# Eight modulation blocks multiplied inside the recurrent scan instead of in the readout after it, and the readout's squares on ScalarE

## What is computed

```python
def adaln(cond, w, b):
    return jnp.split(jax.nn.silu(cond) @ w + b, 6, axis=-1)
...
        h_l = modulate(x, sh_a, sc_a)
...
        x = x + gt_a * o_l
        x = x + gt_m * squared_relu_mlp(modulate(x, sh_m, sc_m), mlp_w1[layer], mlp_w2[layer])
```

```python
    def step(s, inp):
        rt, wt, kt, vt, at, bt = inp
        sa = jnp.einsum('bhij,bhj->bhi', s, at)
        s = s * wt[:, :, None, :] + sa[..., None] * bt[:, :, None, :] + vt[..., None] * kt[:, :, None, :]
        y = jnp.einsum('bhij,bhj->bhi', s, rt) if with_out else None
...
        mean = jnp.mean(y, axis=-1, keepdims=True)
        var = jnp.mean(jnp.square(y - mean), axis=-1, keepdims=True)
        y = ((y - mean) * lax.rsqrt(var + RW_GN_EPS)).reshape(r.shape) * lnx_w + lnx_b
        return ((y + bonus) * g).astype(h_l.dtype) @ w_o
```

## Time and profile before

| | us |
|---|---|
| median of 3 executions | 3275.87 (3272.88 to 3277.51) |
| the profiled execution | 3276.72 |
| its span, first to last instruction | 3274.6 |
| scan, first matmul to last result | about 998 to 1527 |
| readout, to the first matmul of the phase after it | 1527 to 1576.4 |

### The profile page before, as it was taken

How to read it: one execution, slowest core, us unless ns; L and a number is a source line. 1 busy time by engine, 2 the same in 40 slices (tenths; PEclk the granted TensorE clock), 3 DMA queues, 4 the chain that set the end, 5 groups by cost and what they waited for, 6 DMA issues and landing times. The chain is left out here.

```text
span 3274.6 us, 79289 instructions
## 1 busy us (share of the span) xinstructions
PE 2935.4 (90%) x35148; PEld 1967.2 (60%) x35148; DVE 1331.3 (41%) x2021; ACT 948.7 (29%) x1646; POOL 314.5 (10%) x253
## 2 busy tenths in 40 slices
PE   7988899999997788787899988798999998998996
PEld 5865577888575666665799877675333333333332
DVE  3355544333763654555455676464110110110112
ACT  3124433222343333432444563432100100100101
POOL 0021200000321122122000002310000000000001
PEclk9999899999998999999899998988999999999997
DMA  7262412222153100003555432088999999999996
GB/s 267 78 243 78 171 52 103 99 82 103 64 195 114 55 23 23 29 29 109 211 180 181 158 129 81 9 293 306 374 421 421 421 422 421 421 422 421 421 422 265
DMA packets 195063, 681.03 MB, mean 208 GB/s; under 512 B 25616, under 2 KB 40464, under 8 KB 145312
## 3 DMA queue, kind: packets, MB, share of 16 engines
q1 hardware_dynamic: 175328, 651.93, 51.2%
q10 hardware_dynamic: 18336, 21.21, 1.8%
q0 software_dynamic: 1152, 4.19, 0.4%
HBM read 651.86 MB, written 25.43 MB: 207 GB/s over the span
## 5 line engine op out<-in xcount | busy, mean ns | idle before, releaser
L4006 PE MATMUL experts_psum_gu<-ring,experts_x 128*32 128x512 f32 x3840 | 431.4, 597 | 34.6 <-DMA ring<-in_w_gu 34.6
L4128 DVE TENSOR_SCALAR experts_gate<-experts_psum_gu 128x768 f32<-128x768 f32 (+1 forms) x32 | 26.4, 824 | 850.2 <-PE experts_psum_gu L4006 850.2
L4006 PEld LDWEIGHTS experts_psum_gu<-ring,experts_x 128*32 128x32 f32 x3840 | 111.9, 110 | 336.2 <-issue 241.5
L4035 PE MATMUL experts_psum_down<-down_weights,experts_hiddenT 128*32 128x256 f32 x4096 | 231.2, 381 | 15.6 <-DMA down_weights<-in_w_down 12.7
L4035 PEld LDWEIGHTS experts_psum_down<-down_weights,experts_hiddenT 128*32 128x32 f32 x4096 | 127.5, 110 | 128.1 <-DMA down_weights<-in_w_down 32.9
L4072 ACT ACTIVATE experts_sigmoid<-experts_gate 128x768 f32<-128x768 f32 (+1 forms) x32 | 23.6, 737 | 584.9 <-DVE experts_gate L4128 584.9
L991 PE MATMUL mlp_psum_bank<-mlp_x_high,mlp_w_high 128*128 128x512 f32 (+1 forms) x512 | 175.5, 343 | 7.1 <-DVE ring_rounded L315 4.5
L315 DVE TENSOR_TENSOR ring_rounded<-ring,mlp_w_high 128x1024 fp32r<-128x1024 f32 x128 | 156.8, 1225 | 44.4 <-ACT mlp_w_high L310 44.4
L991 PE MATMUL mlp_psum_bank<-xT_rounded,mlp_w_high 128*128 128x512 f32 (+1 forms) x512 | 173.5, 339 | 0.0
L1001 PE MATMUL mlp_psum_bank<-mlp_hidden_high,mlp_w_high 128*128 128x512 f32 (+1 forms) x512 | 172.2, 336 | 1.2 <-ACT mlp_relu L937 1.2
L991 PE MATMUL mlp_psum_bank<-mlp_x_high,ring_rounded 128*128 128x512 f32 (+1 forms) x512 | 173.1, 338 | 0.0
(11 more groups left out here) (793 smaller groups left out, 6052.5 us busy)
## 6 DMA issues: line engine op xcount, KB each, us to landing
ring<-in_w_gu SPq DMA_DIRECT2D x192, 1024.0 KB, 25.9
down_weights<-in_w_down SPq DMA_DIRECT2D x96, 1024.0 KB, 27.2
ring<-in_ada_w SPq DMA_DIRECT2D x72, 1024.0 KB, 10.8
ring<-in_mlp_w SPq DMA_DIRECT2D x64, 1024.0 KB, 7.0
xT<-in_w_gu SPq DMA_DIRECT2D x64, 1024.0 KB, 26.0
ring<-in_w_in SPq DMA_DIRECT2D x24, 1024.0 KB, 6.4
spare_unit<-in_w_down SPq DMA_DIRECT2D x16, 1024.0 KB, 27.1
x<-in_w_down SPq DMA_DIRECT2D x16, 1024.0 KB, 27.3
```

What stands on the lines that cost most here:

```text
L4006: mm = nc.tensor.matmul(pg[32 * j:32 * j + 32, gr, :, :], x, strip(w, j), start=False, stop=(u == U - 1))
L4035: mm = nc.tensor.matmul(pd[32 * c:32 * c + 32, gr, :], hidT[:, a, gr, GROUP * v:GROUP * v + GROUP], w[:, a, C * c:C * c + C], start=(v == ...
L4128: v.tensor_scalar(G, pg[:, 0:groups, 0, :], SWI_LIMIT, None, ALU.min).then_inc(s_gt, 1)
```

## The change

The class `ScanModulate` splits a modulation block into products, copy, fold and keep, and the scan calls these at fixed places. Block 0 is multiplied at the start while the first tile is prepared; block i + 1 is multiplied in the `carry` of step i, between L2217 and L2225. ScalarE copies its result behind its copies of W. The fold of block i is issued at the head of the next `totals`, or at k = 2 of the last step, and ScalarE keeps the folded columns at k = 2. TensorE waits for the copied row at the end of `carry`, and for the kept columns before `cumulate`. SyncE issues one ring unit behind the v load of each step from step 1 on, and one more at the end, so that the next phases' first three units (two of w_o, one of the MLP) are also loaded during the scan.

In the readout the eight blocks go. `ModulateBias` loads the bias behind the other loads and adds it between the reciprocal and the token work. The two squares move from VectorE to ScalarE. The `keep_busy` matmuls go to a bank of their own, six at the start and eight between the two turned tiles.

Apart from that, `keep_busy` is taken out of `gemm_feat` (5 matmuls; it runs as "about" and "rwout"), `mlp` (2 + 4; it runs twice), `ab_merge` (4) and `gemm_rows` (5; "mixout").

```diff
@@ -628,7 +628,6 @@
                     if kt == KT - 1:
                         ring.mark(mm)
 
-                keep_busy(g, banks[:, 0, 0:256], 5)
                 for c in range(CHUNKS):
                     ring.take(pe)
                     for kt in range(KT - 2):
...
                                            ALU.add).then_inc(self.s_end, 1)
+        dve.wait_ge(self.s_end, len(self.parts))
+
+
+class ScanModulate:
+
+
+    def __init__(self, g, ph, parts, each):
+        self.g, self.ring, self.each = g, g.ring, each
+        self.dst = [(g.mods[layer % 2], 4 * f, layer) for layer, first, n, _ in parts for f in range(first, first + n)]
+        self.row = ph.sb("mod_row", [P, each, 512])
+        self.s_row, self.s_fold, self.s_kept = ph.sem("mod_row"), ph.sem("mod_folded"), ph.sem("mod_kept")
+        self.done0 = self.ring.done
+
+    def products(self, pe, n, dst):
+        wv = self.ring.take(pe)
+        for kt in range(KT):
+            j = 32 * (kt % 4)
+            if kt == KT // 2:
+                self.ring.wait(pe, self.ring.used - 1, 1)
+            mm = self.g.nc.tensor.matmul(dst[j:j + 2, :], self.g.silu[:, self.dst[n][2] // 2, kt, :], wv[:, kt, :],
+                                         start=(kt < 4), stop=(kt >= 4))
+        self.ring.mark(mm)
+
+    def copy(self, act, n, src):
+        act.wait_ge(self.ring.gemm_done, self.done0 + n + 1)
+        if n >= self.each:
+            act.wait_ge(self.s_fold, n - self.each + 1)
+        self.g.nc.scalar.copy(self.row[:, n % self.each, :], src).then_inc(self.s_row, 1)
+
+    def fold(self, pe, n, dst):
+        pe.wait_ge(self.s_row, n + 1)
+        for f in range(4):
+            mm = self.g.nc.tensor.matmul(dst[:, 2 * f:2 * f + 2], self.row[:, n % self.each, f * P:(f + 1) * P], self.g.fold[:, :],
+                                         start=True, stop=True)
+        mm.then_inc(self.s_fold, 1)
+
+    def keep(self, act, n, src):
+        act.wait_ge(self.s_fold, self.each * (n // self.each + 1))
+        mods, first, _ = self.dst[n]
+        self.g.nc.scalar.copy(mods[:, first:first + 4, :], src.rearrange("p (a b) -> p a b", b=2)).then_inc(self.s_kept, 1)
+
+
+class ModulateBias:
+
+
+    def __init__(self, g, ph, parts):
+        self.g, self.parts = g, parts
+        self.bias = ph.sb("mod_bias", [P, 4 * sum(n for _, _, n, _ in parts)])
+        self.s_b, self.s_end = ph.sem("mod_bias"), ph.sem("mod_added")
...
@@ -1008,9 +1070,7 @@
                     weights.take(pe, FT + f)
                     pe.wait_ge(s_hl, f + 1)
 
-                keep_busy(g, banks[:, 0, 0:256], 2)
                 xs.spread(pe)
-                keep_busy(g, banks[:, 0, 0:256], 4)
                 ring.take(pe)
                 fs = kts = 0
                 for kind in ARRIVALS:
...
             def _(pe):
-                keep_busy(g, ps[:, 0, 0:256], 4)
                 for k in range(m.n):
                     m.step(pe, k)
                 for t in range(TT):
...
@@ -2011,6 +2070,10 @@
         s_mv, s_mvc, s_w, s_wc, s_u, s_uc = two("MV"), two("MV_copied"), two("W"), two("W_copied"), two("U"), two("U_copied")
         s_pt, s_ptc, s_g, s_gc, s_qt, s_qtc = two("PT"), two("PT_copied"), two("G"), two("G_copied"), two("QT"), two("QT_copied")
         s_ch, s_s, s_y0, s_y, s_yo, own = n("chain"), n("state"), two("y_local"), two("y"), two("y_out"), n("v_chain")
+        s_zero = n("modulation_zero")
+        sm = ScanModulate(g, ph, modulate, 1)
+        mod_at = lambda e: banks[e][:, 0, :]
+        fold_at = lambda e: banks[0][:, 3, 16 + 8 * e:24 + 8 * e]
         steps = [(0, t) for t in (0, 1, 2, 3)] + [(1, t) for t in (1, 0, 3, 2)]
         N = len(steps)
         lat = lambda i: steps[i][1] >= 2
...
                     if i:
                         sync.dma_start(vs[i % 2], scr["v"][t]).then_inc(s_ldv, 16)
+                    g.ring.issue(sync, sm.each * i)
...
 
+                def modulate_step(i):
+                    for e in range(sm.each):
+                        sm.products(pe, sm.each * i + e, mod_at(e))
+
+                def folds(i):
+                    for e in range(sm.each):
+                        sm.fold(pe, sm.each * i + e, fold_at(e))
+
                 def logits(i, which):
 
                     d, t = steps[i]
@@ -2106,6 +2179,8 @@
                 def totals(i):
 
                     take(s_sa, 2)
+                    if i:
+                        folds(i - 1)
                     for kt in range(M8):
                         mm = nc.tensor.matmul(banks[0][:, 3, 2 * kt:2 * kt + 2], at[i % 2][:, kt * P:(kt + 1) * P],
...
                                 mm.then_inc(s_pt[c], 1)
+                    if i + 1 < N:
+                        modulate_step(i + 1)
                     for m in range(M8):
                         for c, l in QUADS:
                             if m == 0 and c == l:
...
+                    if i + 1 < N:
+                        pe.wait_ge(sm.s_row, sm.each * (i + 2))
 
                 def read(i):
 
...
                 cumulate(0)
+                pe.wait_ge(s_zero, sm.each)
+                modulate_step(0)
                 take(s_til)
                 nq = 4 if lat(0) else 3
                 for q in range(nq):
+                    if q == 1:
+                        pe.wait_ge(sm.s_row, sm.each)
                     if q >= 2:
                         turned(0, q - 2, q - 1)
                     turn_in(0, q)
...
                             totals(i + 1)
+                        elif k == 2:
+                            folds(i)
+                        if k == 3:
+                            pe.wait_ge(sm.s_kept, sm.each * (i + 1))
                         if nxt and k == 3:
                             cumulate(i + 1)
...
                 exp_a(0)
+                for e in range(sm.each):
+                    sm.copy(act, e, mod_at(e))
                 turned(0, 0, 4 if lat(0) else 3)
                 for i in range(N):
                     nxt = i + 1 < N
...
                                 exp_a(i + 1)
+                        if k == 2:
+                            for e in range(sm.each):
+                                sm.keep(act, sm.each * i + e, fold_at(e))
                         for l in range(2):
                             take(s_yr[l])
...
                         copy(lanes(at[i % 2][:, :])[:, :, l, :], banks[l][:, 0, :], s_w[l], s_wc[l])
+                    if nxt:
+                        for e in range(sm.each):
+                            sm.copy(act, sm.each * (i + 1) + e, mod_at(e))
                     for c in range(2):
                         copy(T[c][:, :, :], banks[c][:, 3, :], s_g[c], s_gc[c])
                     if nxt:
...
 
+                for e in range(sm.each):
+                    v.memset(mod_at(e), 0.0).then_inc(s_zero, 1)
                 mix_k(0)
                 mix_b(0)
                 before(0)
...
         s_tok, s_tr, s_ev = ph.sem("tile_done"), ph.sem("turned"), ph.sem("turned_copied")
-        m = Modulate(g, ph, *modulate)
+        idle = ph.ps("idle", [P, 512])
+        s_mid, s_sq = ph.sem("centred"), ph.sem("squared")
+        m = ModulateBias(g, ph, modulate)
         with nc.Block() as block:
             @block.sync
             def _(sync):
...
                 fetch.issue(sync)
-                m.ring.issue(sync, m.n)
+                m.sync(sync)
 
             @block.tensor
             def _(pe):
-                keep_busy(g, ps[:, 0, 0:256], 4)
-                m.step(pe, 0)
-                m.step(pe, 1)
+                keep_busy(g, idle[:, 0:256], 6)
                 gates.wait(pe)
                 cells = [(2 * t + j, slice(t * P, (t + 1) * P), slice(512 * j, 512 * j + 512)) for t in range(2) for j in range(2)]
                 for i, rows, cols in cells:
...
 
-                for k in range(2, m.n - 1):
-                    m.step(pe, k)
                 turned(0)
-                m.step(pe, m.n - 1)
+                keep_busy(g, idle[:, 0:256], 8)
                 turned(1)
 
             @block.scalar
             def _(act):
-                for k in range(2):
-                    m.copy(act, k)
+                for t in range(2):
+                    act.wait_ge(s_mid, t + 1)
...
 
-                for k in range(2, m.n - 1):
-                    m.copy(act, k)
-                turned(0)
-                m.copy(act, m.n - 1)
-                turned(1)
+                for t in range(2):
+                    turned(t)
                 act.wait_ge(s_ev, 4)
 
             @block.vector
             def _(dve):
...
                     yt = y[:, t, :]
                     ch.link(nc.vector.tensor_reduce(st[:, 0, c], heads(yt), AX.X, ALU.add))
                     ch.link(nc.vector.tensor_scalar(st[:, 0, c], st[:, 0, c], 1.0 / RW_D, None, ALU.mult))
-                    ch.link(nc.vector.tensor_tensor(heads(yt), heads(yt), rep(st[:, 0, c], RW_D, 2), ALU.subtract))
```

(11 more changed lines are left out.)

22 lines of the change are left out of this document (17 added, 5 removed).

## The result

| kernel | median us | lowest | highest |
|---|---|---|---|
| before | 3273.28 | 3268.02 | 3284.48 |
| after | 3283.34 | 3272.98 | 3294.91 |

The changed kernel takes 1.0029 times as long as the one before (95% interval 1.0018 to 1.0039): 9.5 us slower, 5.9 to 12.8, where the forecast was 0.9 faster.

The account below looks back on a forecast made before the run. The readout was taken to wait for weight transfers, the scan to be TensorE-bound with DMA queues empty. Scan folds 7.8, products 2.0, transfers 5.5 and constant matmuls 1.4, less readout 17.6, gave -0.9: 3275.0 us, range 3264 to 3286.

Parts of the forecast that it names:

- Readout: Between scan and "rwout": without blocks VectorE's chain sets the time, tokens start when the bias lands; gain 17.6 us, bounds 16.5 to 19.5.
- Folds and products: In the scan: folds on the path cost 7.8 us (6 to 8.4); products mostly fill carry gaps, 2.0 (1 to 10.7).
- rival (c): Carry of the scan: blocks don't fill the instruction gaps, so products cost 10.7 instead of 2.0; 3284 us; chance 0.11.
- Transfers: Eight 2 MB units in the scan each delay one instruction batch at half price; cost 5.5 us, bounds 0 to 14.
- Rival (b): Ring transfers starve TensorE of instructions at the scan's 64 x 64 products and read; +7.6, 3283.5 us; chance 0.15.
- rival (a): In the scan nothing but the folds: transfers land in waits, blocks fill fetch gaps; 3267 to 3269 us; chance 0.30.
- Constant matmuls: Removing keep_busy: merge gains 2.0 us, "rwout", "about" and "mixout" start colder; net cost 1.4, bounds -2 to 3.
- the middle case: Whole kernel by the prediction's own sum, with a late bias counted in: 3270 to 3282 us; chance 0.44.

## Why the prediction was wrong, step by step

**Readout: right.** VectorE's reduction starts at 1551.91, the bias comes at 1563.19, 11.3 later; forecast was 1529.3 to 1539.9, 10.6. The token work lasts from 1563.52 to 1577.96 + 1.28, 15.7, as forecast. The squares hide. From the scan's end to the first product of "rwout" 54.3 became 36.2, a gain of 18.1; forecast was 17.6, and 0.8 of the constant matmuls there.

**Folds and products: mechanism right, size not settled.** 7.8 + 2.0 forecast; between two runs 10.1 by the ratios, 6.5 by the medians, 4.3 in the profiled scans. The mechanism of the products is in the rows of after's level 2 and of its carry of step 2:

```profile
1171.77 1.05 PE L791 MATMUL rwkv_psum_lane<-fold,rwkv_mod_row 128*128 128x2 f32 x8
1172.68 2.12 PE L2185 MATMUL rwkv_psum_lane<-rw_shared,rwkv_A 128*128 128x2 f32 x16
...
1199.92 2.30 PE L778 MATMUL rwkv_psum_lane<-ring,silu 128*2 128x512 f32 x16
...
1204.93 0.34 PE L2306 MATMUL rwkv_psum_lane<-x,rwkv_K 64*64 64x64 f32 x7 [0.76 <-issue]
...
1208.78 0.39 PE L2330 MATMUL rwkv_psum_lane<-x,rwkv_mat_KR 64*64 64x64 f32 x6 [0.91 <-issue]
```

Before had gaps of 1.59, 1.93 and 1.56 in this carry; with the block (2.30 long here, 1.90 in the other steps' carries) two of 0.76 and 0.91 are left. In the waits above the gaps of L2225, L2229 and L2240 are 15.5 us in sum before; without transfers the same three (L2301, L2305, L2318) are 3.8. So the blocks fill the gaps, and rival (c) falls. The "mostly hidden" of the Trainium skill ("Runtime: NRT & Kernel Launch", section "Instruction fetch mechanics") doesn't hold here: by it there would have been no gaps to fill. Part comes back one batch later, ahead of the first products of a tile: 8.0 before, 11.9 without transfers (10.4 in the run without blocks, so hardly more than two traces differ). A fold takes 1.05 and totals follow without a gap, as forecast.

**Transfers: the step that failed.** "I take one batch at half price, 0.7: 5.5" was 19.7, beyond the upper end of 14 (alone in the kernel before, 11.1). Rival (b) had mechanism and sign right, with +7.6 against 9.5 measured, and I gave it 0.15. It also said that it decides only from 13 batches, 18 us, on; by my own sum 13 us of transfers, 9 to 10 batches, are enough for +6.5. Two things were mis-sized in the term. First, the row used was a batch that ran beside k and kk (5.4 instead of 4.0 us). I priced the ring's load as one more of these, but it stands behind them and v, so one batch waits for most of the sum: the five long gaps are 1.9 to 3.0 us longer than at the same places without transfers, 13 in all. What had to be read was how many MB are queued when TensorE asks, and that the tile's loads already cost that wait in before (L2142, 8.0 us). Second, a gap was priced at its own length. Behind each of the five the products run at half speed, which at three of the places is the transfers' doing. I had priced that for the constant matmuls and not for the scan. And the "5% busy" of rival (a) was the scan's last stretch, where few tiles are loaded; over the whole scan of before it is 11%.

**Constant matmuls: wrong by little.** Forecast +1.4, measured 0 within 6. Block 0 of the merge starts at 380.63 instead of 382.71, waiting for the memset as forecast, 0.4 later than 380.2. The product behind the merge starts 2.0 earlier, as forecast, but ends only 0.7 earlier (L374 behind it starts at 452.60 instead of 453.28), so the colder clock cost 1.3 there and not 0.6:

```profile
380.63 1.89 PE L745 MATMUL abmerge_psum_mod_row<-ring,silu 128*2 128x512 f32 x8 [5.14 <-DVE abmerge_psum_mod_row L720]
```

"mixout" starts colder, but at a mean clock of 0.72 over its first 6 us (2174 to 2180), which costs at most 0.28 x 6 = 1.7 and shows as 47.1 instead of 46.9 us for the whole product.

**The sum.** Measured between runs: -20.3 for readout and constant matmuls, +10.1 for products and folds, +19.7 for the transfers, together +9.5. Forecast: -16.2, +9.8, +5.5. The 14.2 of the transfers, less 4.1 of the first, and 0.3 of the second are the 10.4 by which the forecast was off. Only the first of these is larger than the uncertainty of its run. The range of 3264 to 3286 held the median; the middle case, 3270 to 3282, didn't.

**What stays open.** Whether the readout, merge and rest are worth 20.3 and not 16.2 (the interval reaches 16.0, the medians give 17.6); what a transfer costs where the ends of batches fall elsewhere; and how the 19.7 divide between gap and clock in a typical execution, since only one execution of each kernel has a trace.

## What to carry to other kernels

A weight transfer moved under a stretch of many small matmuls isn't free because DMA is 5 or 11% busy there. TensorE's own instructions come through the same 16 DMA engines, one batch per 256, and wait behind data that is queued when they are asked for. Look how many MB stand in the queues at that moment, keep it small (pieces that wait for one another, begun when the other loads have landed), and move only as much as the stage that gives it up needs: here five of the eight blocks could stay, and the readout took 38.3 us instead of 36.1.

## What the runs showed of the hardware

- A batch of 256 TensorE instructions is a DMA packet of 16 KB on a queue of its own, and is delayed by data on other queues: 1.88 to 4.90 us of idle at the same place.
- TensorE ran dry at a batch's end although nothing else held it, in before too (gaps of 1.6 to 1.9). The Trainium skill ("Runtime: NRT & Kernel Launch", section "Instruction fetch mechanics") gives TensorE room for 2048 instructions; no lead of that size shows in these traces: in after a packet had moved by 1075.5, the next came at 1085.5, and TensorE had nothing left from 1083.1 on.
- A gap of TensorE of 3.7 to 4.9 us was followed by the lower clock each time, a shorter one in some places and not in others (0.57 behind 1.88 us without transfers, 1.00 behind the 1.93 of the earlier trace rows).
- Time goes loosely with the mean granted clock from one execution to the next: of after's 19, those at 0.951 took 3276.7 to 3278.8 us and the one at 0.944 took 3292.1, but those at 0.948 took 3275.2 to 3283.3. Which of the two drives the other isn't shown. After spreads more than before: 22 us from lowest to highest, against 16.5.
